# A state-space opening on one Trainium2 core: one F group and seven E halves on GpSimd, V ahead of K by two pairs, values kept in PSUM, and Toeplitz rows copied through two DMA queues

## The reference

```python
h = rmsnorm(x, norm_mix)                      # x: 256 tokens, 1024 features
dt = exp(log_dt); ab = exp((lam_re + i lam_im) * dt)     # 64 groups, 64 states
bb = (ab - 1) / lam * b                       # b: (64, 64, 16), complex
bu = einsum('blgh,gph->blgp', h, bb)
xs = associative_scan(ab * left + right, bu)  # along the 256 tokens
y = einsum('blgp,ghp->blgh', xs, c).real + d_skip * h
y = gelu(y)
a, g = split(y @ w_glu, 2);  x = x + a * sigmoid(g)      # w_glu: 1024 x 2048
x = x + sqrelu_mlp(rmsnorm(x), w1, w2);  ...
```

## Time and profile before

| | |
|---|---|
| median of 3 runs | 1971.04 us (1968.45 to 1972.79) |
| the profiled execution: its own time | 1965.51 us |
| its span | 1963.7 us |
| TensorE busy | 1908.0 us (97%) |
| VectorE busy | 919.7 us (47%) |
| ScalarE busy | 756.6 us (39%) |
| GpSimd busy | 1103.0 us (56%) |
| chain that ended last | PE 87%, DVE 7%, ACT 2% |
| end of the last F step of group 0 | 29.6 us |
| first product with `toep` | 97.41 us |
| first matmul of the GLU product | 117.45 us |

### The profile page before, as it was taken

The page is one execution under the profiler, slowest core; times in us unless marked ns, Lnnn a source line. Parts: engine busy times, 40 slices in busy tenths (PEclk is TensorE's granted clock), DMA queues, the critical chain, the costliest instruction groups (busy, mean ns, idle before and its releaser), DMA issues.

```text
span 1963.7 us, 31592 instructions
## 1 busy us (share of the span) xinstructions
PE 1908.0 (97%) x13129; PEld 1639.0 (83%) x13129; DVE 919.7 (47%) x1688; ACT 756.6 (39%) x1212; POOL 1103.0 (56%) x611
## 2 busy tenths in 40 slices
PE   9999999989999999999999999999999999999997
PEld 5588999878887788778878888888788987989997
DVE  7955552363935783742253111114476756262112
ACT  5343453332325522733323222222335536434443
POOL 7345997563535443434443444444468754868885
PEclk8999999989999999999999999999999999999999
DMA  8867766664122132124333323223535331675653
GB/s 195 235 222 235 258 213 234 228 220 159 51 89 65 33 128 65 33 65 140 129 119 118 97 81 123 86 75 112 198 123 148 120 107 44 214 236 174 192 169 100
DMA packets 289491, 276.61 MB, mean 141 GB/s; under 512 B 19802, under 2 KB 276324, under 8 KB 289092
## 3 DMA queue, kind: packets, MB, share of 16 engines
q1 hardware_dynamic: 286804, 271.42, 43.6%
q10 hardware_dynamic: 2192, 2.77, 0.4%
q0 software_dynamic: 352, 0.40, 0.1%
HBM read 266.70 MB, written 4.19 MB: 138 GB/s over the span
## 4 chain that ended last, share of the span: by engine, by line
PE 87%; DVE 7%; ACT 2%; issue 2%; DMA 1%; POOL 1%; SPq 1%; ACTq 0%; DVEq 0%; POOLq 0%
PE gb L2610 19%; PE gb L2611 19%; PE gb L2612 19%; PE gb L1761 3%; PE gb L1759 3%; PE gb L1760 3%; PE gb L1487 3%; PE gb L1489 3%; PE gb L1488 3%; PE mb L1208 1%; PE mb L667 1%; PE gb L667 1%; DMA raw<-in_w_ada 1%; PE mb L1275 1%; DVE mx L1237 1%
## 5 line engine op out<-in xcount | busy, mean ns | idle before, releaser
L2597 POOL TENSOR_TENSOR wl<-raw,wh 128x1024 fp32r<-128x1024 f32 (+3 forms) x448 | 972.8, 2190 | 777.3 <-ACT wh L819 777.2
L819 ACT CAST wh<-raw 128x1024 fp32r<-128x1024 f32 (+3 forms) x452 | 420.1, 939 | 658.2 <-PE gb L2612 381.3
L2610 PE MATMUL gb<-xh,wh 128*128 128x256 f32 (+1 forms) x1856 | 602.1, 324 | 8.4 <-DVE xl L1158 4.6
L2611 PE MATMUL gb<-xl,wh 128*128 128x256 f32 (+1 forms) x1856 | 598.2, 322 | 0.0
L2612 PE MATMUL gb<-xh,wl 128*128 128x256 f32 (+1 forms) x1856 | 598.2, 322 | 0.0
L2610 PEld LDWEIGHTS gb<-xh,wh 128*128 128x128 f32 x1856 | 350.4, 189 | 44.3 <-issue 11.1
L2612 PEld LDWEIGHTS gb<-xh,wl 128*128 128x128 f32 x1856 | 350.4, 189 | 27.6
L2611 PEld LDWEIGHTS gb<-xl,wh 128*128 128x128 f32 x1856 | 350.5, 189 | 27.1
L1759 PE MATMUL gb<-fhh,wh 128*128 128x512 f32 (+1 forms) x352 | 118.4, 336 | 0.0
L1761 PE MATMUL gb<-fhh,wl 128*128 128x512 f32 (+1 forms) x352 | 117.9, 335 | 0.0
L1760 PE MATMUL gb<-fhl,wh 128*128 128x512 f32 (+1 forms) x352 | 117.9, 335 | 0.0
(11 more groups left out here) (478 smaller groups left out, 3009.5 us busy)
## 6 DMA issues: line engine op xcount, KB each, us to landing
raw<-in_w_in SPq DMA_DIRECT2D x62, 1024.0 KB, 5.3
raw<-in_w_ada SPq DMA_DIRECT2D x48, 1024.0 KB, 5.4
raw<-in_w_ffn SPq DMA_DIRECT2D x44, 1024.0 KB, 5.2
raw<-in_mlp_w SPq DMA_DIRECT2D x32, 1024.0 KB, 5.6
raw<-in_w_ffn SPq DMA_DIRECT2D x16, 768.0 KB, 4.6
...
```

The costliest lines, as they stand in the source:

```text
L819: nc.scalar.copy(split_half(wh, p, j, h), raw_half(p, it, j, h)).then_inc(hi_ready, 1)
L2597: nc.gpsimd.tensor_tensor(split_half(wl, p, j, h), raw_half(p, it, j, h), split_half(wh, p, j, h).bitcast(F32), ALU.subtract)\
L2610: nc.tensor.matmul(o, H[:, k, :], XH, start=st, stop=False)
L2611: nc.tensor.matmul(o, H[:, k, :], XL, start=False, stop=False)
```

## The change

- GpSimd makes F for the second F group (`f_half(1, 0)` and `f_half(1, 1)`) directly after `Db`, and then seven E halves in place of five; VectorE keeps F groups 0, 2 and 3 and the half (2,1). The memory of the groups is exchanged for that (`Fg`). The scaling of `U` stands inside `f_group(2)`, behind its first product.
- TensorE transposes two pairs of F at a time and multiplies two pairs at a time; ScalarE copies two pairs in one instruction. K comes after V without ada blocks in between; the ada blocks 2 to 6 come after K. Some `warm` products are added early, and the 13 ahead of `y_products` become 3.
- The scan's temporaries and factors, and the values y and g of the GELU, are in PSUM.
- SyncE issues four of the seven Toeplitz copies and ScalarE three. The block ada 4 has memory of its own (`beside_ring`, at the end of E) and leaves the ring, so the ring's list is one shorter before the GLU blocks.
- ScalarE's first four `split_hi` stand in the GELU's loop, at d = 4 to 7, and GpSimd makes the matching `wl` in place of VectorE. The ada blocks 8 to 13 are multiplied after d = 0, 1, 5, 6, 7 and 7. The GLU product waits for seven of the eight x tiles.

```diff
-        Fg = [F[:, 0], F[:, 1], F2, F3]
+        Fg = [F[:, 0], F3, F[:, 1], F2]
-        EARLY_ADA, EARLY_GLU = 10, 2
-        RINGSEQ = [("ada", n) for n in range(EARLY_ADA)]
+        EARLY_ADA, EARLY_GLU, BESIDE = 10, 2, 4
+        RINGSEQ = [("ada", n) for n in range(EARLY_ADA) if n != BESIDE]
         RINGSEQ += [("w", p_glu, i) for i in range(EARLY_GLU)]
         RINGSEQ += [("ada", n) for n in range(EARLY_ADA, FIRST_ADA)]
-        TOEP_AT = 12
+        TOEP_AT = 6
+        TOEP_SP = 4
...
+        def toep_dma(eng, lags):
+            eng.wait_ge(s_Kc, 2)
+            for j in lags:
                 low = GH * (CH - 1 - j)
-                sp.dma_start(toep[low:P, j, :, :], toep[0:P - low, CH - 1, :, :]).then_inc(s_T, 16)
+                eng.dma_start(toep[low:P, j, :, :], toep[0:P - low, CH - 1, :, :]).then_inc(s_T, 16)
...
@@ scalar @@
-            for q in range(PAIRS):
-                act.wait_ge(s_w1t, q + 1)
-                if q >= 4:
-                    act.wait_ge(s_w1u, q - 3)
-                nc.scalar.copy(w1[:, q % 4, :, :], gb[:, 1 + q % 2, 0:256].rearrange("p (r m) -> p r m", r=2))\
-                    .then_inc(s_w1, 1)
+            for b in range(PAIRS // 2):
+                act.wait_ge(s_w1t, b + 1)
+                if b >= 2:
+                    act.wait_ge(s_w1u, b - 1)
+                nc.scalar.copy(w1[:, 2 * (b % 2):2 * (b % 2) + 2, :, :],
+                               gb[:, 1 + b % 2, :].rearrange("p (e r m) -> p e r m", e=2, r=2)).then_inc(s_w1, 1)
...
-            for j in range(EARLY_GLU):
-                if j == 1:
-                    act.wait_ge(s_E, 4)
-                    act.wait_ge(s_S, 1)
-                for h in range(2):
-                    split_hi(act, (p_glu, 0, j), h)
+            toep_dma(act, range(TOEP_SP, CH - 1))
...
             for d in range(KD):
                 gelu_square(d)
                 if d:
                     gelu_hi(d - 1)
                 gelu_tanh(d)
+                if d >= 4:
+                    if d == 6:
+                        act.wait_ge(s_E, 4)
+                        act.wait_ge(s_S, 1)
+                    split_hi(act, (p_glu, 0, (d - 4) // 2), d % 2)
@@ gpsimd @@
+            def f_half(r, ri):
+                q = slice(8 * r, 8 * r + 8)
+                shape = [P, 8, CH - 1, GH]
+                pj = [pw[:, 1:CH, k, q].rearrange("p j q -> p q j").unsqueeze(3).to_broadcast(shape) for k in range(2)]
+                lw = [Bb[:, k, q, :].unsqueeze(2).to_broadcast(shape) for k in range(2)]
+                tmp = tE[:, 0:8 * (CH - 1) * GH].rearrange("p (q j h) -> p q j h", q=8, h=GH)
+                dst = Fg[r][:, :, ri, 1:CH, :]
+                P1.add(g_.tensor_tensor(dst, pj[0], lw[ri], ALU.mult))
+                pstep(g_.tensor_tensor(tmp, pj[1], lw[1 - ri], ALU.mult))
+                pstep(g_.tensor_tensor(dst, dst, tmp, (ALU.subtract, ALU.add)[ri]))
-            pool.wait_ge(s_Ctc, 2)
             pool.wait_ge(s_Bb, 1)
-            pool.wait_ge(s_U, 1)
-            e_half(0, 0)
+            f_half(1, 0)
+            f_half(1, 1)
+            pool.sem_inc(s_Fp, 1)
             pool.wait_ge(s_th, 1)
...
+            pool.wait_ge(s_Ctc, 2)
+            pool.wait_ge(s_U, 1)
+            for r in range(4):
+                if r == 3:
+                    pool.wait_ge(ada_used, BESIDE + 1)
+                e_half(r, 0)
+                if r != 2:
+                    e_half(r, 1)
+                pool.sem_inc(s_E, 1)
@@ tensor @@
-            warm(2, 2)
+            warm(3, 2)
...
-            for q in range(PAIRS + 1):
-                if q < PAIRS:
-                    w1_transposes(q)
-                if q:
-                    v_products(q - 1)
-                if q in (8, 12, 16, 20):
+            for b in range(PAIRS // 2 + 1):
+                if b < PAIRS // 2:
+                    w1_transposes(b)
+                if b:
+                    v_products(b - 1)
+                if b in (8, 12):
...
             for d in range(KD):
                 y_products(d)
-                late = ((0,), (1,), (), (2,), (), (), (), (3,))[d]
-                for b in late:
-                    ada_block(pe, EARLY_ADA + b)
-                if not late and d < KD - 1:
-                    warm(1, 1)
+                late = ((8,), (9,), (), (), (), (10,), (11,), (12, 13))[d]
+                for n in late:
+                    ada_block(pe, n)
+                if not late:
+                    warm(1, 2)
+            pe.wait_ge(s_xl, KD - 1)
@@ vector @@
             f_group(0)
             dve.wait_ge(s_ss, 1)
             rsqrt(D1, ss[:, 1, :], ss[:, 2, :], ss[:, 3, :], ss[:, 0, :], ss[:, 0, :], 1.0 / D, EPS)
...
-            f_group(1)
-            f_group(2)
+            f_group(2, scale_u)
             f_group(3)
             dve.wait_ge(s_Ctc, 2)
             e_beside(2, 1)
-            e_beside(3, 0)
```

237 lines of the change are left out of this document (119 added, 118 removed).

## The result

| | before | changed |
|---|---|---|
| median | 1970.61 us of 4 runs (1968.45 to 1972.79) | 1989.38 us of 4 runs (1987.81 to 1989.95) |
| ratio | | 1.0090, 95% interval 1.0071 to 1.0108 |
| span of the profiled execution | 1963.7 us | 1988.0 us |
| mean granted clock | 0.992 | 0.981 |

The change costs 18.8 us. The forecast was +8.9 us, 1980 with a range of 1970 to 1987: the right side, half the size, and the measured time lies outside the range.

A forecast was written before the change was run, and what follows sets the result against it. TensorE, busy 97% of the span, was taken as the bound, so only the start before the GLU product counted: 9.5 - 5.9 - 3.2 - 2.6 + 9.6 + 1.5 = +8.9 us on 1971.0, say 1980 us, range 1970 to 1987.

The forecast's parts named there:

- Part 1: Opening: GpSimd's F products beside the root hold VectorE's small steps, so `chk` and the first F transpose come later, +9.5 us.
- Rival A: Opening: the root's small steps slip between GpSimd's instructions and are not held; total -0.6 us, 1970.4 us; chance 0.15.
- Part 2: V stage: transposing and multiplying two pairs per step, at 1.2 us a step, shortens V, -5.9 us.
- Part 3: K stage: K directly behind V, with three ada blocks of 1.0 us each moved behind it, -3.2 us.
- part 6: Start of the GLU product: TensorE idles some 10 us before it, so it starts at 1.2 GHz, +1.5 us.
- rival C: Before y: the clock falls there as well, adding 4 us to the 8.9, 1984 us; chance 0.15.
- Part 4: K's last copy to first y product: no load ahead, Toeplitz issues split over two queues; 12.1 us, -2.6 us.
- Part 5: y stage: the last ada block's load waits for late rounding and subtraction, delaying the GLU product, +9.6 us.
- Rival B: End of y: the last ada block is not late and the clock stays up; total -2.2 us, 1968.8 us; chance 0.10.

The follow-up runs named there:

- held_on_before: Kernel before, plus six GpSimd products of an F group made beside the root, result thrown away: 1986.7 us, ratio 1.0083.
- f_behind_root: Changed kernel, with GpSimd's F group waiting for `chk` so that it no longer runs beside the root: 1987.6 us, ratio 1.0077 to before.
- The two kernels on before: Kernel before with only V in steps of two pairs: 1971.6 us; the same plus two warm groups ahead of V's fifth step: 1970.2 us.
- blocks_in_k: Changed kernel, with ada blocks 2, 3 and 4 moved from behind K to three places in it: 1989.6 us, ratio 1.0087 to before.
- loads_before: Changed kernel, ada blocks 2 to 4 within K and loads of ada 7 and 8 ahead of the Toeplitz copies: 1987.5 us, ratio 1.0084 to before.
- combined: Changed kernel: GpSimd's F behind root, four warms out, ada 2-4 in K, ada 7-8 loads before Toeplitz copies, splits at d 1-4: 1975.2 us.
- combined_ring: combined, but ada 10 and 11 ahead of the first GLU weights in the ring, splits at d = 5 to 7 and after: 1972.0 us.
- ada7_first: Changed kernel, with ada 7's load issued ahead of SyncE's four Toeplitz copies instead of behind them: 1995.1 us, ratio 1.0108 to before.
- one_queue: Changed kernel, with all seven Toeplitz copies issued by SyncE and none by ScalarE: 1988.6 us, ratio 1.0089 to before.

## Why the prediction was right and where it failed

**Part 1, the held root: right.** +9.5 forecast, +8.1 measured. One step was held per GpSimd instruction, 1.65 to 1.94 us each, as the earlier trace rows had it; five steps were held and not six (beside the first instruction only the root's first step was late, 0.28 us for 0.17). held_on_before shows that in the kernel before the way from there to the end has no slack, f_behind_root that in the changed kernel most of it does have: the warms and the transposes at half clock stand right behind. Rival A, the root not held, is out.

**Part 2, V: right in the change, -7.2 for -5.9**, with steps of 1.17 us where 1.2 was taken. The two kernels on before add that it holds only with F off VectorE.

**Part 3, K: the step that failed first.** The prediction took the three ada blocks out of K and subtracted their 3.2 us; it measured +3.1, a miss of 6.3 us. `k_back` alone took 3.3 us more (7.09 against 3.79), the skip gain's products ran in part at half clock (2.63 us against 1.98), and the two pauses took 2.4 us, where the kernel before has one of 0.25. blocks_in_k gives the clock and the 3.79 back and shortens the pauses to 0.8 us, so taking the blocks out is what cost them here. The kernels with the same blocks and longer pauses (loads_before, combined, combined_ring) lose the clock again, so the blocks are not the whole cause. The prediction looked at the clock at the end (part 6) and before y (rival C) and not in K, where it removed the wide work.

**Part 4, the copies: failed by 5.2 us,** +2.6 for -2.6. Its 12.1 us is right for the copies alone (12.6 in loads_before). What the step named and then priced too low is ada 7's load, which "comes right behind SyncE's four and shares the engines": its product waited until 102.31 and ran at half clock. The upper bound of 15.5 for this stage was too low as well. That load is what stood there: with ada 7 and 8 loaded before the copies the stage took 12.6 us (loads_before), and with ada 7 merely put ahead of them 18.0 (ada7_first). The second queue, which the prediction counted in this term, brought nothing (one_queue).

**Part 5, the y stage: right in kind, 3.8 us too small,** +13.4 for +9.6. The chain is the one that was written down, and its sizes are off: from the last transpose (123.27) 3.25 to the end of the rounding (3.12 forecast), 2.76 for the remainder (2.49), 6.36 for the load (5.08) and 1.87 for the product (1.0, at half clock), 14.2 in place of 11.9. Up to the last transpose it was 19.3 us and not 17.7; the clock was 0.52 from 104 to 108. Rival B, the last ada block in time, is out.

**Part 6 and rival C, the clock.** The GLU product did start at 0.50: from its first product to its sixth 1.2 us pass, 0.7 in the kernel before (the second comes after 0.38, the others 0.16 to 0.22 apart) where 0.12 each is usual. So this term measured some 0.5 us and not 1.5; the 3 us at the lower level that it took stood in no row. Ada 13's product at half clock, 0.9 us more, came on top, in part 5. Rival C had the clock fall before y too, and it did (0.50 from 100 to 104), but it held for the first rounds only. E's two added halves were costed at nothing, and no product waited for them, though GpSimd ended E at 102.3 us and not by 95: its last two halves wait for ada 4, which came at 88.18.

So the signs of parts 1, 2, 5 and 6 were right, those of 3 and 4 wrong, and these two alone miss by 11.5 us. Part 5 adds 3.8, and parts 1 and 2 take 2.7 back: 12.6, from the +7.4 that parts 1 to 5 give at the start of the GLU product to the +20.0 measured there (137.5 us, for the forecast's 123 to 128). Behind it part 6 gives back 1.0. What the medians show of the whole is 18.8 us.
